# Attention in a hybrid encoder block: the value product as three products of high and low halves

## The reference, cut to what matters

```python
def attend_block(args):
    qn, qr, bi = args                                   # a block of 128 queries
    s = (jnp.einsum('bqhd,bkhd->bhqk', qn, k_nope)
         + jnp.einsum('bqhr,bkr->bhqk', qr, k_rope)).astype(jnp.float32) * sm_scale
    q_chunk = (bi * Q_BLOCK + jnp.arange(Q_BLOCK)) // CHUNK
    allowed = k_chunk[None, :] <= q_chunk[:, None]
    s = jnp.where(allowed[None, None], s, NEG_INF)
    p = jax.nn.softmax(s, axis=-1).astype(v.dtype)
    return jnp.einsum('bhqk,bkhd->bqhd', p, v)
```

## Time and profile before

| | us |
|---|---|
| median of 3 runs | 2076.04 (2073.07 to 2079.74) |
| profiled execution, whole time | 2077.84 |
| its span | 2076.0 |
| attention stage, first to last instruction, about | 664 |
| one of the 8 heads in the loop | 77.0 |

### The profile page before, as it was taken

How to read it: one execution, slowest core, us unless ns; L and a number is a source line. 1 busy time by engine, 2 the same in 40 slices (tenths; PEclk the granted TensorE clock), 3 DMA queues, 4 the chain that set the end, 5 groups by cost and what they waited for, 6 DMA issues and landing times. The chain is left out here.

```text
span 2076.0 us, 27000 instructions
## 1 busy us (share of the span) xinstructions
PE 1865.4 (90%) x8674; PEld 1447.5 (70%) x8674; DVE 1284.9 (62%) x2171; ACT 693.5 (33%) x1106; POOL 484.6 (23%) x540
## 2 busy tenths in 40 slices
PE   2899999997999999999996999972999999999980
PEld 2677777764666666666664788862899999999960
DVE  5687878956876876876875656545244444444444
ACT  3544443314344434434433332320222222222214
POOL 0131313102211211211211111100234343434320
PEclk9999999997999999999998899985899999999995
DMA  7656555530000000000002444414599999999958
GB/s 271 196 151 178 150 171 153 143 95 0 6 9 6 10 5 6 10 5 6 10 5 95 173 143 147 152 72 146 190 272 275 271 273 274 274 274 273 276 112 325
DMA packets 213570, 290.81 MB, mean 140 GB/s; under 512 B 23829, under 2 KB 167408, under 8 KB 213242
## 3 DMA queue, kind: packets, MB, share of 16 engines
q1 hardware_dynamic: 190906, 220.60, 32.2%
q0 software_dynamic: 20224, 69.22, 13.3%
q10 hardware_dynamic: 2368, 0.17, 0.1%
HBM read 229.13 MB, written 60.82 MB: 140 GB/s over the span
## 5 line engine op out<-in xcount | busy, mean ns | idle before, releaser
L895 PE MATMUL tbank<-probs,VV 128*128 128x512 f32 (+3 forms) x640 | 292.1, 537 | 1.2 <-ACT probs L1109 1.2
L1109 ACT ACTIVATE probs<-tbank 128x512 f32<-128x512 f32 (+1 forms) x320 | 170.2, 532 | 248.1 <-PE tbank L866 243.1
L977 DVE TENSOR_REDUCE cmax<-tbank 128x1 f32<-128x512 f32 (+2 forms) x340 | 204.2, 601 | 73.6 <-PE tbank L820 67.4
L377 PE MATMUL pbank<-hhi,wslhi 128*128 128x512 f32 x512 | 208.8, 408 | 12.2 <-DVE wsllo L428 11.2
L1850 DVE TENSOR_SCALAR xTe<-ebank,modcol 128x256 f32<-128x256 f32 (+1 forms) x128 | 53.7, 473 | 263.1 <-PE ebank L1770 138.8
L864 PE MATMUL tbank<-Qhi,Khi 97*128 97x512 f32 (+2 forms) x321 | 212.4, 662 | 0.0
L377 PE MATMUL pbank<-hhi,wsllo 128*128 128x512 f32 x512 | 202.3, 395 | 0.0
L377 PE MATMUL pbank<-hlo,wslhi 128*128 128x512 f32 x512 | 202.1, 395 | 0.0
L1135 POOL TENSOR_SCALAR diag<-cst,nmax 128x128 fp32r<-128x128 f32 x138 | 84.1, 610 | 490.9 <-DVE nmax L980 490.6
L1792 PE MATMUL ebank<-xTe,wg 128*128 128x192 f32 x1024 | 174.7, 330 | 3.1 <-DVE ahi L1878 1.8
L1792 PEld LDWEIGHTS ebank<-xTe,wg 128*128 128x128 f32 x1024 | 170.8, 193 | 7.9 <-DVE ahi L1878 2.1
(11 more groups left out here) (271 smaller groups left out, 3487.7 us busy)
## 6 DMA issues: line engine op xcount, KB each, us to landing
wg<-in_w_exp_gate SPq DMA_DIRECT2D x32, 1024.0 KB, 5.7
wu<-in_w_exp_up SPq DMA_DIRECT2D x32, 1024.0 KB, 9.4
wd<-in_w_exp_down SPq DMA_DIRECT2D x32, 1024.0 KB, 7.6
wraw<-in_w_in SPq DMA_DIRECT2D x60, 512.0 KB, 4.1
wmod<-in_w_ada POOLq DMA_DIRECT2D x64, 256.0 KB, 3.4
wada<-in_w_ada SPq DMA_DIRECT2D x2, 4096.0 KB, 20.1
xt<-in_x SPq DMA_DIRECT2D x4, 2048.0 KB, 12.4
mixed<-mix_dram SPq DMA_DIRECT2D x16, 512.0 KB, 4.3
```

The source lines that it names most:

```text
L377: ins = pe.matmul(out, w[:, S % 3, k], h[:, n % 2, k], start=k == 0 and j == 0, stop=k == KD - 1 and j == 2)
L895: ins = pe.matmul(out, VV[:, kt, 2 * b:2 * b + 2].rearrange("p c d -> p (c d)"), step_of(probs, m), start=kt == 0, stop=last)
L977: W(ve.tensor_reduce(cmax[:, i % 2, n:n + 1], plain[:, chunk % 2, 0:w], AX.X, ALU.max), plain_read)
L1109: A(act.activation(step_of(probs, m), scores[:, m % 2, j * P:512], ACT.Exp), exp_done)
```

## The change

The values are no longer kept as float32 `VV` but as two halves, `VVhi` (rounded by ACT, L1095 after the change) and `VVlo` (the rest, by DVE, `lower_values`, L1008), both in the type with one pass a product. The probabilities are treated alike: ACT takes the exponential of each step twice, once rounded into `phi` (L1150) and once in float32 into `probs` (L1151), which now lies in the buffer of `KR`. POOL subtracts one from the other into `plo` (`prob_low`, L1177). Both are rings of four steps (`RING`).

PE's value product becomes three: `VVhi` by `phi` and `VVlo` by `phi` in step m, and `VVhi` by `plo` for step m - 2 (`LAG`), so it ends a group two steps later. `copy_out` and one of the `divide` groups move by the same two steps, and `make_values` too. The diagonals leave POOL: DVE makes each one right after its `nmax`, with a wait between them (L1002). Before the loop, a product by zero sets the bank that a memset had set, and ACT fills the blocks of ones and zeros.

```diff
-V_AT = [(1, STEPS_HEAD - NT + 4 * (v + 1)) if v < V_PARTS - 1 else (0, 1) for v in range(V_PARTS)]
+LAG = 2
+RING = 4
+V_AT = [(1, STEPS_HEAD - NT + 4 * (v + 1) + LAG) if v < V_PARTS - 1 else (0, LAG + 1) for v in range(V_PARTS)]
-                                        (1, (18, 19, 20, 22)), (2, (28, 29, 30, 31)))
+                                        (1, (18, 19, 20, 22)), (2, (29, 30, 32, 33)))
...
+            def value_low(m, b, first):
+                g, kt = STEP_OF[m]
+                last = kt == GQ * (g + 1) - 1
+                pe.wait_ge(plo_done, first + (m + 1 + RING))
+                ins = pe.matmul(outp[:, g % 2, first_tile(g, kt) * P:512], heads_values(VVhi, kt, b),
+                                step_of(plo, m), start=False, stop=last)
+                if last:
+                    ins.then_inc(out_done, 1)
...
                     def value(m):
-                        pe.wait_ge(exp_done, hp * 2 * STEPS_HEAD + (b * STEPS_HEAD + m + 1))
+                        pe.wait_ge(phi_done, hp * 2 * STEPS_HEAD + (b * STEPS_HEAD + m + 1))
...
-                        ins = pe.matmul(out, VV[:, kt, 2 * b:2 * b + 2].rearrange("p c d -> p (c d)"),
-                                        step_of(probs, m), start=kt == 0, stop=last)
-                        if last:
-                            ins.then_inc(out_done, 1)
+                        pe.matmul(out, heads_values(VVhi, kt, b), step_of(phi, m), start=kt == 0, stop=False)
+                        pe.matmul(out, heads_values(VVlo, kt, b), step_of(phi, m), start=False, stop=False)
...
                         value(m)
+                        if m >= LAG:
+                            value_low(m - LAG, b, hp * 2 * STEPS_HEAD + b * STEPS_HEAD)
+                        else:
+                            value_low(m - LAG + STEPS_HEAD, 1 - b, hp * 2 * STEPS_HEAD + (b - 1) * STEPS_HEAD)
...
# DVE
-                    W(ve.tensor_reduce(nmax[:, i:i + 1], cmax[:, i % 2, 0:n + 1], AX.X, ALU.max, negate=True),
-                      max_ready)
+                    W(ve.tensor_reduce(nmax[:, i:i + 1], cmax[:, i % 2, 0:n + 1], AX.X, ALU.max, negate=True))
+                    W.wait()
+                    W(ve.tensor_scalar(diag[:, i // GQ % 2, i % GQ * P:(i % GQ + 1) * P], cst[:, C_ID:C_ID + P],
+                                       nmax[:, i:i + 1], None, ALU.mult), diag_ready)
+            def lower_values(v, pair, src=made):
+                ve.wait_ge(v_copied, pair * V_PARTS + (v + 1))
+                at = slice(v * 4, (v + 1) * 4)
+                W(ve.tensor_tensor(VVlo[:, at, 0::2], src.rearrange("p (t c d) -> p t c d", c=2, d=VD),
+                                   VVhi[:, at, 0::2].bitcast(F32), ALU.subtract), v_lowered)
...
# ACT, step m
+                        act.wait_ge(plo_done, hp * 2 * STEPS_HEAD + (b * STEPS_HEAD + m + 1))
+                        A(act.activation(step_of(phi, m), scores[:, m % 2, j * P:512], ACT.Exp), phi_done)
                         A(act.activation(step_of(probs, m), scores[:, m % 2, j * P:512], ACT.Exp), exp_done)
-                        if kt == 0:
+                        if kt == LAG:
                             copy_out((g - 1) % GROUPS, hp * 2 + (b if g else b - 1))
...
# POOL
-            def diagonal(i, head):
-                hold(po, max_ready, head * NT + (i + 1), passed_pool)
-                po.tensor_scalar(diag[:, i // GQ % 2, i % GQ * P:(i % GQ + 1) * P], cst[:, C_ID:C_ID + P],
-                                 nmax[:, i:i + 1], None, ALU.mult).then_inc(diag_ready, 1)
+            def prob_low(m, count):
+                hold(po, exp_done, count, passed_pool)
+                po.tensor_tensor(step_of(plo, m), step_of(probs, m), step_of(phi, m).bitcast(F32), ALU.subtract
+                                 ).then_inc(plo_done, 1)
```

More of the change, by code:

```diff
@@ L722, in attend @@
         Khi, Klo = sb("Khi", [P, 2, S], F32R), sb("Klo", [P, 2, S], F32R)
-        VV = sb("VV", [P, NT, 4, VD])
-        probs = sb("probs", [P, 4 * 512])
+        VVhi, VVlo = sb("VVhi", [P, NT, 4, VD], F32R), sb("VVlo", [P, NT, 4, VD], F32R)
+        phi, plo = sb("phi", [P, RING, 512], F32R), sb("plo", [P, RING, 512], F32R)
+        probs = KR[:].rearrange("p (r n) -> p r n", r=RING)
         qf, turned_q = sb("qf", [P, 2, 512]), sb("turned_q", [P, 512])
@@ L912, in _ @@
                             c = PART_AT[m]
+                            if b == 0 and c == 1:
+                                pe.wait_ge(v_lowered, hp * V_PARTS + V_PARTS)
                             if c == 0:
@@ L935, in _ @@
                             spread_maxima(g, nxt if ahead else head)
+            for m in range(STEPS_HEAD - LAG, STEPS_HEAD):
+                value_low(m, 1, (HEADS - 1) * STEPS_HEAD)
         @block.vector
@@ L1016, in _ @@
                   qf_ready)
+                if 0 < n <= V_EARLY:
+                    lower_values(n - 1, 0, bank[:, V_EARLY_BANK[n - 1]])
                 for chunk in range(AHEAD):
@@ L1037, in _ @@
                             part(PART_AT[m], 1 - b, hp * 2 + (b + 1))
+                        if (b, m - 1) in V_AT:
+                            lower_values(V_AT.index((b, m - 1)), hp + b)
                         if m in DIVIDE_AT:
@@ L1096, in _ @@
                 mask_rows(0, n)
+                v, k = (VVhi, VVlo)[n % 2], n // 2 * 2 + 1
+                A(act.activation(v[:, :, k], cst[:, C_ONE:C_ONE + VD].unsqueeze(1).to_broadcast([P, NT, VD]), ACT.Copy,
+                                 scale=1.0 - n % 2), filled)
+            for k in (0, 2):
+                A(act.activation(VVhi[:, NT - LAG:, k], cst[:, C_ONE:C_ONE + VD].unsqueeze(1).to_broadcast([P, LAG, VD]),
+                                 ACT.Copy, scale=0.0), filled)
+            A(act.activation(plo[:, RING - LAG:].rearrange("p r (a n) -> p (r a) n", n=P),
+                             cst[:, C_ONE:C_ONE + P].unsqueeze(1).to_broadcast([P, LAG * 4, P]), ACT.Copy, scale=0.0), filled)
             rope(1)
@@ L1149, in _ @@
                     for m in range(STEPS_HEAD):
-                        chunk, ahead = chunk_at(m)
-                        if chunk in TILE_END:
-                            diagonal(TILE_END.index(chunk), hp * 2 + (b + ahead))
+                        prob_low(m, hp * 2 * STEPS_HEAD + (b * STEPS_HEAD + m + 1))
                         if PART_AT.get(m - QUERIES_REST_AFTER, 0) % 2:
```

50 lines of the change are left out of this document (23 added, 27 removed).

## The result

| | us | |
|---|---|---|
| before, median of 4 runs | 2077.78 | 2073.07 to 2079.74 |
| after, median of 4 runs | 2154.19 | 2152.31 to 2158.86 |
| ratio | 1.0375 | 95% interval 1.0349 to 1.0400 |
| span of the profiled execution | 2152.0 | 2076.0 before |

The change costs 76 us. The direction was forecast, the size was not: 2102 us was the number, and the range ended at 2132.

What follows compares the result with a forecast made beforehand. PE was taken as the bound, with DVE close behind in steps 5 to 24. Stretches of +4.9, -1.0 and -0.9 us gave +3.0 a head, 24 for eight, plus 2 outside: 2102 us, range 2066 to 2132.

Steps and rivals of the forecast that it cites:

- PE bounds, DVE is close behind in steps 5 to 24: PE bounds the old kernel; in steps 5 to 24 DVE becomes the bound, 47.4 us against 42.5.
- DVE's eight diagonals at 0.29 us: Steps 5 to 24 hold 8 of a head's 16 diagonals, adding 2.3 us of DVE work.
- Which instructions are exposed to POOL: Scalings, copies and two-input instructions in SBUF wait for POOL; PSUM readers and the reciprocal don't; 15 exposed in steps 5 to 24.
- The mean wait of 0.35 us: Each exposed DVE instruction waits 0.35 us for POOL, bounds nothing to 1.3; 5.2 us a head in steps 5 to 24.
- POOL has room: POOL's forty subtractions a head fit, 1.30 of 1.64 us in a full step; 27.1 us in steps 5 to 24.
- Steps 25 to 33 at -1.0 us: In this stretch PE would take 14.9 us and DVE 14.3 in bursts, put at 15.3 against 16.3 a head.
- Steps 34 to 4 at -0.9 us: PE alone bounds this stretch and gains 0.75 us a head, taken as 0.9 with the narrow steps.
- PE's gain of 0.15 us a step: In each 512-column step, three one-pass products take 0.70 us where the float32 value product takes 0.85.
- Set-up +0.7 us: Ahead of the loop 4.78 us of DVE idling goes; 7 diagonals, three `lower_values` and waits, some 5.5 us, come.
- The engines miss each other: Rival, 17%: DVE's diagonals always fall in POOL's gaps, no waits, -2.6 us a head, 2057 us.
- The engines lock together badly: Rival, 13%: diagonals come just after POOL starts, waits of 0.8 us; 2165 us at worst, 2135 likelier.
- ACT falls behind: Rival, 8%: ACT waits in order for late rotated queries, delaying the next exponentials, four places a head; about 2120 us.

Runs made afterwards that it cites:

- e4: Changed kernel with each of POOL's subtractions covering only two columns, diagonals still on DVE: 2093.94 us, ratio 1.0079.
- e2: Changed kernel with the 16 diagonals a head made by ACT instead of DVE: 2092.69 us, ratio 1.0082.
- e5: Kernel before the change with only the diagonals moved to DVE, right behind their maximum: 2082.28 us, ratio 1.0032.
- e6: Changed kernel with each of POOL's subtractions of the low probabilities cut into two halves of its columns: 2179.28 us, ratio 1.0503.
- e9: Changed kernel with one of a head's 16 diagonals, the one slow at step 27, made by ACT: 2138.67 us, ratio 1.0305.
- e1: Changed kernel with the value part of step 3 made in the bank `spread` instead of `made`: 2132.66 us, ratio 1.0262.
- e3: Changed kernel with the edits of e1 and e2 together: 2080.38 us, ratio 1.0005 to the kernel before.

## Why the prediction was right or wrong

**PE bounds, DVE is close behind in steps 5 to 24**: right. The stretch was forecast at 47.4 us and took 47.0 (46.2 to 48.1). The sign that was named for it came only in its total. The idle time in front of PE's plain products was forecast at some 5 us a head, in this stretch only. It is 40.4 / 8 = 5.05 us a head, but some 1.8 us of that in steps 5 to 24, 1.6 in steps 25 to 33 and 1.9 in steps 34 to 4; in steps 5 to 24 PE waited as long, 1.6 us a head, in front of L803, which makes queries, for DVE's `Klo`.

**DVE's eight diagonals at 0.29 us**: right alone, 285 to 288 ns at the least in every kernel. The work itself cost 1.2 us (e4 against e2) to 1.5 us (e5), since part of 2.3 us fell into slack.

**Which instructions are exposed to POOL**: right. After the change the reciprocal keeps 943 ns, the instructions that read PSUM keep 0.69 us. The exposed ones grew, the division's product to 1.13 us in the mean:

```profile
L1021 DVE TENSOR_TENSOR on<-raw,rs 64x512 f32<-64x512 f32 x32 | 36.3, 1135 | 1.1
...
L985 DVE TENSOR_TENSOR qf<-qf,turned_q 32x512 f32<-32x512 f32 x32 | 24.1, 754 | 1.1
```

The queries' sum L985 hardly grew (median 683 ns, one of 1816; why, I did not test); its mean of 754 ns just passes the 0.7 us that was named.

**The mean wait of 0.35 us.** Here the first step fails. In steps 5 to 24 the sum came out: the 15 exposed instructions waited 4.7 us a head where 5.2 were forecast. That is in part luck, for 1.1 us of it are the 2.8 us diagonals at step 15, which the step did not allow. In steps 25 to 33 it fails: the term was 5 x 0.35 = 1.75 us, and the four diagonals and one L1021 there waited 6.0 us a head, 4.0 of it in the diagonal at step 27. Over all 138 diagonals, 126 waited 0.33 us in the mean, and the other twelve carry half of all the waiting. The step said "a scaling, a copy or a two-input instruction in SBUF stands until POOL's current one ends", and took 1.3 us as the worst case. That was read from the earlier trace rows, where each wait shown is beside one POOL instruction. But the earlier trace rows had a sign against it: the longest L510 took 1771 ns, more than 0.29 + 1.30. In the trace of the kernel before it starts 0.36 us ahead of POOL's L338, while POOL is busy issuing a transfer (L333), and still stands until L338 has ended:

```profile
118.26 0.57 POOL L333 DMA_DIRECT2D mod_dram<-macc  x1
118.48 1.77 DVE L510 TENSOR_SCALAR macc<-wmod,csil 128x128 f32<-128x128 f32 x1
118.84 1.31 POOL L338 TENSOR_TENSOR hlo<-hf,hhi 128x512 fp32r<-128x512 f32 x1
```

The trace after and e6 show it in full: 4.30 us through three more subtractions and 7.61 us through ten halves. Nor is the rule "until POOL has nothing ready", as the diagonals at 703.76 and, in e6, at 721.44 show. What decides is open. The Trainium skill, "SBUF — State Buffer", section "Who interferes with whom", says that whoever issues first gets the shared pair for the whole instruction and that the other fully blocks. The diagonal at 703.76 agrees, since it ended with that one instruction; at the long waits the trace disagrees, for the block lasted until three or ten more had finished.

**POOL has room**: right as a sum, 26.27 busy of 46.10 us, and wrong as a reason. The step compared 1.30 us of work with a step of 1.64 us and stopped there. It left out what happens behind a low half of the queries: with 0.36 us of room per step, 1.28 us takes 1.28 / 0.36 = 3.6 steps to be made up. That is an estimate for an even supply. The supply is not even either: before the backlog POOL stood idle for 2.81 us (the row at 744.54), because ACT had waited 2.50 us for the queries' sum (it copies `Qhi` at 742.77) and then did its exponentials close together (`KR` ended at 746.57 and 747.55, 0.98 us apart where a full step is some 1.6). How the backlog divides between the two causes no run shows.

**Steps 25 to 33 at -1.0 us**: wrong, +2.5. The one long diagonal at step 27, with what hangs on it, is all of that: e9 takes it away and the stretch is 16.2 us. Without any diagonal on DVE (e2) it is 15.9, 0.5 us of gain, and with POOL's subtractions short (e4) 15.4, the 1.0 us that the sum had.

**Steps 34 to 4 at -0.9 us**: wrong, +3.6, about 29 us over eight heads. This is the second step that fails, "PE alone": steps 34 to 39 fell as it said, and steps 0 to 4 at the loop's entry and turns grew. Three costs were not in the sum. The value part of step 3 was counted only as a `lower_values` "where DVE has room", and PE's side of the same move, a bank taken over from the keys one step before, was left out; e1 gives 21.5 us for it. The doubled work of ACT was found covered by a full step's 1.64 us, which holds, but at the turn of the loop ACT has one exponential more and its instructions stop for 2.28 us ahead of the table load, where in the kernel before they stopped for 0.17 us; PE waits 2.5 us. And after such idle times PE ran at half the granted clock. I did not isolate these last two by runs of their own. Both remain in e3, whose turns take 7.2 us from step 0 to step 3 where the kernel before takes 4.6. The waits of this stretch's diagonals, 2.0 us a head, were not in the sum either, but cost little of the time: with ACT making them (e2) it went only from 21.6 to 21.2 us.

**PE's gain of 0.15 us a step**: right for the instructions. In e3 value passes stand 0.23 us apart and full steps most often 1.62 us. It reached the time only in part: steps 5 to 24 went from 42.6 to 41.9, not to 40.4, because PE waits for DVE's maxima and for `phi` where a key copy stands ahead of it on ACT, in one stretch of 44 us 1.0 + 0.4 us. With the set-up and the turns of the loop against it, e3 comes out level.

**Set-up +0.7 us**: right, from attention's first copy to the loop's it took 44.8 us before and 45.6 after, though I counted 7 diagonals there and there are 10, so the fit of the sum is in part luck.

**The rivals.** "The engines miss each other" assumed no waits, and is out. "The engines lock together badly" had the right direction and not the mechanism: it gave every exposed instruction 0.8 us in steps 5 to 24, where the forecast's own term held, and only "about 1 us" to the next nine. "ACT falls behind" was priced for the queries' copies; it showed at the turn of the loop instead. No rival had a single instruction that waits through several of POOL's, nor the bank.

## What to carry to other kernels

When two engines share a port, don't price the wait by the other engine's current instruction alone: look for the places where it works through several instructions without a gap, for there the wait can be the whole row, and cutting them into shorter ones made it longer here. A mean far above the median in one line's instructions is the mark. And when a step is moved, list for each buffer that it writes who used it last and on which engine's queue the release stands; a move of PE's own small product cost more here (21.5 us) than its change of passes gained (0.7 + 0.5 us a head in e2, some 10 us).

## What the runs showed of the hardware that I had not expected

- A VectorE scaling from SBUF to SBUF can get no turn between GpSimd instructions that follow each other without a gap: 4.30 us over four of 1.28 us, the first of them already half done, and 7.61 us over a row of ten of 0.69 us, once in each of eight heads. A 128x128 scaling on ScalarE took 385 to 403 ns beside the same GpSimd work.
- When it does get a turn is not settled. In the 4.30 us case it ended with GpSimd's third subtraction, at 750.89, while the fourth started at 750.77; the input of that fourth had been ready for only 0.2 us (ACT's exponential ended at 750.54), that of the others for 0.45 to 0.7 us. That would fit "served when GpSimd has nothing waiting". But the diagonal at 703.76 was served ahead of an instruction whose input had been ready for over 2 us, and in e6 36 diagonals were served between the two halves of one subtraction.
- ScalarE's turn of a loop cost 1.8 to 2.3 us without an instruction in the kernels with two exponentials per step, ahead of a 1.28 us table load, and 0.17 us in the kernel before. Why was not tried.
- At the turns of the loop, after 2.1 to 3.2 us without a product, TensorE's granted clock read 0.50 for 3.4 to 6.8 us; in the kernel before, without such an idle time there, it stayed at 1.00. It also fell with less: in the changed kernel it read 0.50 for 3.4 us from 908.6 us on, after two waits of 0.7 and 0.6 us had left PE busy for 0.76 us of the 2 us from 906 to 908.
